# Twelve dummy products between the two pairs of up products, in the late batches of a mixture-of-experts kernel

## What is computed

```python
def one_block(args):
    toks, e = args
    xb = x_pad[toks]
    hb = jax.nn.silu(xb @ w1[e]) * (xb @ w3[e])
    return hb @ w2[e]

y_rows = lax.map(one_block, (row_tok.reshape(n_blk, MOE_BLOCK), blk_exp)).reshape(n_rows, D)
y = jax.ops.segment_sum(y_rows * row_gate[:, None], row_tok, num_segments=T + 1)[:T]
```

## Time and profile before

| | |
|---|---|
| timed runs (3) | median 1150.59 us, 1150.25 to 1151.67 |
| the profiled execution | 1149.66 us |
| its span, first to last instruction | 1147.9 us |
| mean granted clock of TensorE | 0.993 |
| TensorE busy | 1046.3 us, 91% of the span |
| VectorE, ScalarE busy | 403.6 us, 260.3 us |
| moved by DMA | 441.05 MB, mean 384 GB/s |

### The profile page before, as it was taken

The page is one execution under the profiler, slowest core; times in us unless marked ns, Lnnn a source line. Parts: engine busy times, 40 slices in busy tenths (PEclk is TensorE's granted clock), DMA queues, the critical chain, the costliest instruction groups (busy, mean ns, idle before and its releaser), DMA issues.

```text
span 1147.9 us, 26691 instructions
## 1 busy us (share of the span) xinstructions
PE 1046.3 (91%) x11382; PEld 534.3 (47%) x11382; DVE 403.6 (35%) x1189; ACT 260.3 (23%) x683; POOL 18.7 (2%) x36
## 2 busy tenths in 40 slices
PE   9999999989889988888899999989889989988888
PEld 5665753434444443333466657434344444433333
DVE  4865532222222221222268656322222222222213
ACT  1245321111121111111131544121221111111111
POOL 0010000000000000000000100000000000000000
PEclk9999999999999999999999999999999999999999
DMA  9967699999999999999996677999999999999997
GB/s 307 330 249 293 256 400 406 428 426 425 426 428 429 429 429 429 429 429 420 387 319 227 268 297 278 403 426 425 426 426 429 428 428 429 428 429 428 429 421 268
DMA packets 72861, 441.05 MB, mean 384 GB/s; under 512 B 16480, under 2 KB 36064, under 8 KB 43616
## 3 DMA queue, kind: packets, MB, share of 16 engines
q1 hardware_dynamic: 72512, 439.52, 93.6%
q0 software_dynamic: 144, 0.58, 0.1%
q10 hardware_dynamic: 144, 0.07, 0.0%
HBM read 439.10 MB, written 1.05 MB: 383 GB/s over the span
## 4 chain that ended last, share of the span: by engine, by line
PE 73%; SPq 9%; DMA 9%; DVE 6%; issue 2%; ACT 1%; POOL 0%; DVEq 0%
PE bank L1087 13%; PE bank L1172 12%; PE bank L1184 8%; PE bank L693 8%; DMA w_odd<-in_moe_w 8%; PE bank L1069 7%; SPq L401 5%; PE bank L819 4%; PE bank L1102 3%; SPq L540 3%; PE bank L1137 2%; PE bank L1178 2%; DVE moe L1745 1%; PE bank L1056 1%; PE bank L963 1%
## 5 line engine op out<-in xcount | busy, mean ns | idle before, releaser
L1808 ACT ACTIVATE moe<-bank 128x512 f32<-128x512 f32 (+2 forms) x164 | 84.2, 523 | 555.8 <-PE bank L1087 275.5
L1709 DVE COPY moe<-bank 128x512 f32<-128x512 f32 x64 | 44.3, 692 | 315.6 <-PE bank L1087 256.9
L1184 PE MATMUL bank<-moe 128*128 128x512 f32 (+1 forms) x264 | 119.3, 593 | 23.6 <-DVE moe L1745 22.5
L1172 PE MATMUL bank<-w_even,moe 64*32 64x512 f32 x896 | 99.0, 590 | 10.1 <-DVE moe L1729 10.1
L1087 PE MATMUL bank<-w_odd,moe 64*32 64x512 f32 x1536 | 92.8, 629 | 11.2 <-issue 6.1
L1069 PE MATMUL bank<-moe,x 128*64 128x64 f32 x3072 | 98.3, 224 | 2.6 <-issue 2.6
L1069 PEld LDWEIGHTS bank<-moe,x 128*64 128x64 f32 x3072 | 94.8, 138 | 6.8 <-issue 6.8
L1745 DVE COPY moe<-bank 128x512 f32<-128x512 f32 x32 | 22.1, 692 | 198.7 <-PE bank L1172 178.0
L1184 PEld LDWEIGHTS bank<-moe 128*128 128x128 f32 x264 | 47.3, 190 | 96.0 <-DVE moe L1745 48.9
L1172 PE MATMUL bank<-w_odd,moe 64*32 64x512 f32 x768 | 84.8, 590 | 7.5 <-DVE moe L1729 7.5
L1087 PE MATMUL bank<-w_even,moe 64*32 64x512 f32 x1536 | 86.1, 591 | 5.9 <-issue 5.9
(11 more groups left out here) (203 smaller groups left out, 1013.5 us busy)
## 6 DMA issues: line engine op xcount, KB each, us to landing
w_even<-in_moe_w SPq DMA_DIRECT2D x76, 2048.0 KB, 36.4
w_odd<-in_moe_w SPq DMA_DIRECT2D x72, 2048.0 KB, 34.3
w_odd<-in_moe_w SPq DMA_DIRECT2D x44, 1024.0 KB, 10.2
w_even<-in_moe_w SPq DMA_DIRECT2D x40, 1024.0 KB, 9.6
w_even<-in_w_in SPq DMA_DIRECT2D x24, 768.0 KB, 11.0
w_odd<-in_w_out SPq DMA_DIRECT2D x4, 2048.0 KB, 13.6
w_odd<-in_moe_w SPq DMA_DIRECT2D x8, 512.0 KB, 11.1
w_even<-in_w_in SPq DMA_DIRECT2D x4, 416.0 KB, 6.8
```

What stands on the lines that cost most here:

```text
L1172: last = mm(bank[h][BLK * k:BLK * (k + 1), :], hT_pair[rows, c, BLK * q:BLK * (q + 1)], w2_pairs[parity][q][rows, c, 512 * h:512 * h + 512 ...
L1184: return mm(Y[t][h][:, lo - 512 * h:hi - 512 * h], scatter[:, t * P:(t + 1) * P], y_rows[:, lo:hi], start=False, stop=True, skip_group_che ...
L1709: nc.vector.tensor_copy(partial[:, k, :], source[:, :]).then_inc(part_dve.sem, 1)
L1808: return fn(dst, src, ACT.Copy)
```

## The change

`batch` gets an argument `warm`. If it is not zero, so many dummy products into bank 2 are issued after the up products of the first pair and before those of the second. They wait for nothing. The loop over batches 4 to 13 becomes two loops with bodies of their own: one over 4 to 9 as before, one over 10 to 13 with `warm=12`. Batch 14 gets `warm=12` too. The other engines' programs are as before.

```diff
--- before.py
+++ after.py
@@ -1223,11 +1223,13 @@
                     pe.wait_ge(y2_act.sem, b0 + 1)
                     add_all()
 
-                def batch(j, parity, seen=None, pairs=True, next_pairs=True):
+                def batch(j, parity, seen=None, pairs=True, next_pairs=True, warm=0):
                     b = b0 + (j + parity)
                     pe.wait_ge(xg_dve.sem, b + 1)
                     if seen is None:
                         for q in range(NB // 2):
+                            if q and warm:
+                                keep_warm(warm, bank[2])
                             up_gate_pair(j, parity, q)
                     else:
                         for k in range(NB):
@@ -1296,10 +1298,13 @@
                 batch(0, 1, 32 + 32 * l, pairs=False, next_pairs=False)
                 batch(2, 0, 48 + 32 * l)
                 batch(2, 1)
-                with pe.Fori(4, m, 2) as j:
+                with pe.Fori(4, BATCHES - 6, 2) as j:
                     batch(j, 0)
                     batch(j, 1)
-                batch(m, 0, next_pairs=False)
+                with pe.Fori(BATCHES - 6, m, 2) as j:
+                    batch(j, 0, warm=12)
+                    batch(j, 1, warm=12)
+                batch(m, 0, next_pairs=False, warm=12)
                 last_batch(m)
                 if l < DEPTH - 1:
                     keep_warm(9)
```

## The result

The changed kernel takes 1157.64 us (median of 5 runs, 1155.61 to 1159.75) against 1150.59 us before: ratio 1.0056, 95% interval 1.0036 to 1.0075. It is slower by 7.05 us. Its profiled execution took 1157.64 us too, with a span of 1155.8 against 1147.9.

What follows compares the result with a forecast made beforehand. Weight transfers set the pace, with TensorE close behind and tied at each layer's end. Dummy overrun 3.2 + second loop 2.0 = 5.2 us on 1149.66 gave 1154.9; half of the timed runs' 0.93 made it 1155.3, range 1152.0 to 1160.0.

Steps and rivals of the forecast that it cites:

- the mechanism that was foretold: Batches 10 to 14: dummy delays add up, TensorE never catches up with the weights; layer 1's second pair is 1.05 us late.
- TensorE's path ties at the end of the layer.: Last batch's down products: VectorE's copy ties with the transfer, so lateness at batch 14's second pair reaches the layer's end.
- T = 2.86 us.: Cost of one place of twelve dummies between the two pairs, ways in and out included; bounds 2.68 and 3.1 us.
- Stalls in the new body, 1.2 per layer.: New code of batches 10 and 11: one TensorE stall of 1.2 us per layer; bounds none and two of 1.60.
- a gain that I had put at 0.4: Layer 2, batches 4 and 5: shifted code may stall less than the present 2.48 us; 0.4 us taken as gain.
- The clock drops cost nothing.: Two batches per layer: dummies remove drops of 1.70 us each, costed at nothing because weight waits already hide them.
- the third rival: Timed runs also drop the clock at batch 14, where it counts; dummies save 1.70 us per layer: 1147.2 us; chance 0.03.
- "The transfers behind keep their times.": Weight transfers in both layers: with a deep queue, a buffer freed 2 or 3 us later is not missed.
- 2.13 from the dummies: Layer 2: with five places of dummies batch 14's second pair starts at 1097.43 against weights at 1095.30, 2.13 us late.
- "I am wrong if an idle gap is left before batch 14's second pair.": Sign against the forecast: with idle time left before batch 14's second pair, the layer's end cannot move.
- 2.0 for it: Second loop's new code, both layers: stalls of 1.2 + 1.2 less a gain of 0.4, 2.0 us.
- 3.2 without the stalls: Dummies' overrun at batch 14's second pair: 1.05 us in layer 1 and 2.13 in layer 2, together 3.2 us.

Runs made afterwards that it cites:

- the moved kernel: The change with 16 more dummies at the very start, moving all later code by 64 instructions: 1156.65 us, ratio 1.0045 against the kernel before.
- three loops: Against the kernel before: batches 4 to 7, 8 to 11, and 12 and 13 in three loops in place of one, no dummies: 1157.67 us, ratio 1.0051.

## Why the prediction was right, and where it was off

The sum was 5.2 us, the forecast 1155.3 us and slower; 1157.64 came, 7.05 over the median before and inside the range. Layer 1 went by the mechanism that was foretold. Layer 2 did not: its number, 2.9 foretold and 3.27 measured, is close by luck. By the prediction's own steps:

- **TensorE's path ties at the end of the layer.** Right: 4.84 us at batch 14's second pair became 4.86 at 570.17, and in layer 2 8.14 became 8.13.
- **T = 2.86 us.** 3.0 was measured (steps of 29.14 and 29.04 in place of 26.13 and 26.00). The row of 24 is 2.94 long; the ways in and out are nearly twice what I took. Five places give 15.1 in place of 14.3, so 0.8 of the miss per layer, where TensorE is the bound.
- **Stalls in the new body, 1.2 per layer.** In layer 1 there were two, which lengthened batches 10 and 11 by 1.37 and 1.38: 2.75, and the sum closes: 407.37 + 104.26 + 3.47 + 15.1 + 2.75 = 532.95, measured 532.93. In layer 2 there were none, nor in its batches 4 and 5, a gain that I had put at 0.4. That the place of the code against its pieces decides is shown by the moved kernel and by the stall of batch 5, which stands at the same instruction in seven kernels.
- **The clock drops cost nothing.** Right for batches 11 to 13: the changed kernel has no drop there and gains nothing. Wrong as a general statement: a drop in batch 14, or in batch 0 of layer 2, is on the path and costs 1.7 us or more. The change did not prevent the latter. The timed runs of the kernel before seem to have such drops too, as the third rival suspected: of the 47 beside the experiments the 13 with a granted clock of 0.991 or less average 1152.9 us, the 11 with 0.995 or more 1148.7. The changed kernel's five stand at 0.996 to 0.999, so that its 7.05 us may be a larger loss less some 2 us given back; no run separates the two. The rule of the Trainium skill (TensorE: Matmul & The Clock Gate, section Why this matters for your kernels), that no idle gap is to stand between bursts, spoke for a gain. With three dummies in every batch, which fit, the ratio is 1.0008, so no run here shows a gain on balance.
- **"The transfers behind keep their times."** This is the step that failed, and with it the way in which layer 2 was summed. I had layer 2 at 2.13 from the dummies and 0.8 from the new code (1.2 less 0.4), all on TensorE; it was 3.27, and TensorE was not the bound. By its own steps alone TensorE would have reached batch 14's second pair at 979.30 + 104.26 + 3.47 + 15.1 = 1102.13, and it started at 1103.44. The weights were late, 8.14 us against before. Their first part landed at 1097.51 in place of 1091.43, 6.08 later: 4.86 of the layer's own start and 1.2 of the transfers that ran dry behind the clock drop of batch 0. The last part came another 2.06 later, because the landings were 5.84 apart in place of 3.78; 1.6 of this is the second loop's step, and the rest was there before it. In layer 1 the same lateness (6.00 in place of 3.87) was hidden behind TensorE. The trace before had the sign of it: across the one loop's first turn its landings go from 2.26 to 3.83 us apart, and the prediction priced new code by TensorE's stalls alone.
- **"I am wrong if an idle gap is left before batch 14's second pair."** By this sign layer 2 fails: 0.81 us of idle time are left in batch 12 and 0.22 in batch 14. The reason given with it, that then the layer's end cannot move, took the weights' times as fixed.
- **The two halves of the loss.** The runs with the split alone (3.3 us) and with eight dummies (3.8 us over the runs beside it) show that about half of the 7 us is the second loop, with intervals of 1.7 to 5.1 and 2.2 to 4.9 us. The prediction had 2.0 for it, as stalls on TensorE; it is mostly a lateness of weights. The other half is the overrun with its stalls, for which I had 3.2 without the stalls.

Nor does any run show why a layer starts with 1.9 us or with 4.2, as the kernel with three dummies does in layer 1, which reaches 5.84 without a second loop. That the drop of the clock in batch 0 of layer 2 has to do with the change is not shown: it stood in the profiles of the change, the split alone, eight dummies and the moved code, and not in those of the other four experiments and of the kernel before.

## What to carry to other kernels

A filler in a wait is free only as long as the sum of the work from the last point where the engine was ahead still arrives in time; compare starts along the whole stretch, not the filler with one wait. A loop that is split has a price of its own: its first turn must be fetched, which can stall a dense run of small instructions, and behind it the last part of every transfer lands later (1.5 us here) for as long as the queue stays full. Where transfers set the pace, a clock drop costs only where no wait behind it takes it up. And weights that come later make TensorE's waits longer, with which a drop can come at a place where it counts.

## What the hardware showed that I had not expected

- The 16 parts of one 2 MB transfer land up to 7.1 us apart when the queue is full (three loops, layer 2), and the distance stays for hundreds of us: 3.83 at 293 us and 3.87 at 528 us in the kernel before. It grew in stretches with instruction transfers, by 1.4 to 1.6 us for the first turn of a loop.
- The stall in a gather stands at the same instruction in seven kernels with the same code before it (0.62 to 1.22 us), and it vanishes or appears with 64 instructions of code placed long before it.
- A loop body of two batches with 12 products (24 instructions) more in each was kept and not fetched again; with twice as many it was fetched again in layer 1.
- One clock drop of TensorE in layer 2's first batch goes with weights that come 0.6 to 1.6 us later behind it, in four kernels that have the drop against five that have not.
